# RWKV time mix inside a two-block network: the order of keys, decay, a, receptance, gate and values, scan inputs made during the values' products, mixed inputs kept in PSUM, two units of keys fed together

## The reference

```python
xx = jnp.pad(h, ((0, 0), (1, 0), (0, 0)))[:, :-1] - h
xm = h[None] + xx[None] * mix[:, None, None, :]
xr, xw, xk, xv, xa, xg = xm[0], xm[1], xm[2], xm[3], xm[4], xm[5]
r = xr @ w_r
k = xk @ w_k
v = xv @ w_v
w_log = -jax.nn.softplus(-(w0 + jnp.tanh(xw @ w1) @ w2)) - 0.5
a = jax.nn.sigmoid(a0 + (xa @ a1) @ a2)
g = jax.nn.sigmoid(xg @ g1) @ g2
kk = (k * k_k).reshape(B, T, H, N)
kk = kk / jnp.maximum(jnp.sqrt(jnp.sum(kk * kk, axis=-1, keepdims=True)), 1e-12)
k = k * (1.0 + (a - 1.0) * k_a)
decay = jnp.exp(-jnp.exp(w_log))
y = wkv7_scan(r, decay, k, v, -kk, kk * a)
bonus = (jnp.sum(rh * kh * r_k, axis=-1, keepdims=True) * vh).reshape(B, T, D)
```

## Time and profile before

| | us |
|---|---|
| median of 3 runs (lowest to highest) | 1727.52 (1726.04 to 1730.08) |
| the profiled execution, its own time | 1721.24 |
| its span, first to last instruction | 1719.50 |
| PE busy in the span | 1576.6 |
| DVE busy | 696.7 |
| ACT busy | 738.5 |
| POOL busy | 1089.1 |

### The profile page before, as it was taken

How to read it: one execution, slowest core, us unless ns; L and a number is a source line. 1 busy time by engine, 2 the same in 40 slices (tenths; PEclk the granted TensorE clock), 3 DMA queues, 4 the chain that set the end, 5 groups by cost and what they waited for, 6 DMA issues and landing times.

```text
span 1719.5 us, 40062 instructions
## 1 busy us (share of the span) xinstructions
PE 1576.6 (92%) x15940; PEld 1493.1 (87%) x15940; DVE 696.7 (41%) x1587; ACT 738.5 (43%) x1216; POOL 1089.1 (63%) x552
## 2 busy tenths in 40 slices
PE   6999969649998999999999988999988999879998
PEld 6999969628887999999999986699978987669998
DVE  4332065675445433213332287643341436443300
ACT  5444444423313444444444433654434534445532
POOL 5777848435403777787777752078867863338896
PEclk9999989769997999999999998999999999889999
DMA  6444623200011444454445642044546642215452
GB/s 237 172 178 145 206 101 138 79 0 2 3 52 50 157 178 171 151 199 172 171 148 168 200 149 74 2 157 173 188 115 190 225 146 98 75 53 193 175 210 80
DMA packets 38778, 231.28 MB, mean 135 GB/s; under 512 B 4511, under 2 KB 7680, under 8 KB 17552
## 3 DMA queue, kind: packets, MB, share of 16 engines
q1 hardware_dynamic: 34560, 225.49, 37.4%
q10 hardware_dynamic: 4112, 4.31, 1.3%
HBM read 227.09 MB, written 2.62 MB: 134 GB/s over the span
## 4 chain that ended last, share of the span: by engine, by line
PE 80%; DVE 8%; issue 7%; POOL 4%; ACT 1%; DMA 0%; SPq 0%; DVEq 0%; POOLq 0%; ACTq 0%
PE PS L744 66%; POOL wlo L693 4%; PE PS L743 2%; PE PS L927 1%; PE PS L942 1%; DVE score L2049 1%; PE PS L1296 1%; PE PS L934 1%; DVE prnb L2327 1%; PE PS L1087 1%; ACT whi L2405 0%; PE PS L1078 0%; PE PS L966 0%; PE PS L972 0%; PE PS L1272 0%
## 5 line engine op out<-in xcount | busy, mean ns | idle before, releaser
L693 POOL TENSOR_TENSOR wlo<-raw,whi 128x1024 fp32r<-128x1024 f32 (+1 forms) x472 | 1028.1, 2201 | 539.0 <-ACT whi L2405 486.2
L744 PE MATMUL PS<-xh,whi 128*128 128x272 f32 (+1 forms) x2336 | 681.9, 292 | 52.4 <-POOL wlo L693 23.0
L744 PE MATMUL PS<-xl,whi 128*128 128x272 f32 (+1 forms) x2336 | 674.4, 289 | 0.0
L744 PE MATMUL PS<-xh,wlo 128*128 128x272 f32 (+1 forms) x2336 | 673.6, 288 | 0.0
L2405 ACT ACTIVATE whi<-raw 128x1024 fp32r<-128x1024 f32 (+1 forms) x472 | 449.0, 982 | 281.7 <-PE PS L744 237.5
L744 PEld LDWEIGHTS PS<-xh,whi 128*128 128x128 f32 x2336 | 446.8, 191 | 61.8 <-issue 33.3
L744 PEld LDWEIGHTS PS<-xl,whi 128*128 128x128 f32 x2336 | 448.1, 192 | 0.3
L744 PEld LDWEIGHTS PS<-xh,wlo 128*128 128x128 f32 x2336 | 448.2, 192 | 0.0
L744 PE MATMUL PS<-hid_h,whi 128*128 128x272 f32 (+1 forms) x960 | 276.4, 288 | 16.8 <-POOL wlo L693 16.7
L744 PE MATMUL PS<-hid_h,wlo 128*128 128x272 f32 (+1 forms) x960 | 275.6, 287 | 0.0
L744 PE MATMUL PS<-hid_l,whi 128*128 128x272 f32 (+1 forms) x960 | 274.7, 286 | 0.0
(11 more groups left out here) (379 smaller groups left out, 1602.0 us busy)
## 6 DMA issues: line engine op xcount, KB each, us to landing
raw<-w_f_in_in SPq DMA_DIRECT2D x88, 1024.0 KB, 4.8
raw<-w_f_dn_in SPq DMA_DIRECT2D x64, 704.0 KB, 4.1
raw<-w_b_ff_in SPq DMA_DIRECT2D x32, 1024.0 KB, 4.8
raw<-w_rk_r_in SPq DMA_DIRECT2D x4, 1024.0 KB, 4.9
raw<-w_rk_k_in SPq DMA_DIRECT2D x4, 1024.0 KB, 4.7
raw<-w_rk_v_in SPq DMA_DIRECT2D x4, 1024.0 KB, 4.8
raw<-w_rk_o_in SPq DMA_DIRECT2D x4, 1024.0 KB, 4.9
raw<-w_at_q_in SPq DMA_DIRECT2D x4, 1024.0 KB, 4.9
```

The costliest lines, as they stand in the source:

```text
L693: nc.gpsimd.tensor_tensor(wlo[U % SPL][:, part], raw[U % RAW][:, part], whi[U % SPL][:, part].bitcast(F32), ALU.subtract).then_inc(s_lo, 1)
L744: mm(out, a, b, start=start and n == 0, stop=stop and n == 2, **kw)
```

## The change

The order of stages becomes keys, first factor of decay and a, receptance, second factor, gate, values. Line numbers in the rows below are each kernel's own.

```diff
-    ("rk_r", 4, 4, 2048), ("rk_k", 4, 4, 2048), ("rk_v", 4, 4, 2048),
-    ("lora_wa", 1, 1, 1024), ("lora_g", 1, 1, 1280), ("wa2", 1, 8, 1024),
+    ("rk_k", 4, 4, 2048), ("lora_wa", 1, 1, 1024), ("rk_r", 4, 4, 2048), ("wa2", 1, 8, 1024),
+    ("lora_g", 1, 1, 1280), ("rk_v", 4, 4, 2048),
...
+        def mixed_chunk(c):
+            return PS[:, 4 + c % 4, 0:T]
```

```diff
+                def first_two():
+                    U, G = U0[name], G0[name]
+                    pe.wait_ge(s_lo, 2 * (U + 2))
+                    pe.wait_ge(s_free, G)
+                    for k in range(KC):
+                        pe.wait_ge(s_x, X0[x] + k + 1)
+                        for u in range(2):
+                            for mi in range(2):
...
+                            if k == KC - 1:
+                                last.then_inc(s_unit, 2)
...
-            project("rk_r", T, 0, "m0")
-            project("rk_k", T, 1, "m1")
-            project("rk_v", T, 0, "m2")
+            project("rk_k", T, 1, "m0", wide=True)
...
+            project("rk_r", T, 3, "m3")
...
+            def spread_kk():
+                pe.wait_ge(s_kki, 1)
+                for c in range(KC):
+                    if c >= 4:
+                        pe.wait_ge(s_kkd, c - 3)
...
+            project("rk_v", T, 0, "m5", between=spread_kk)
```

VectorE: mixes are made in halves of four chunks, into PSUM, with four xh/xl buffers (indices 0 to 3; two more lie in tiles that are filled later), between the drains:

```diff
+            MIXES = ((2, 1), (1, 2), (4, 0), (0, 3), (5, 1), (3, 0))
...
-            mix(1, 2)
-            for u in range(4):
-                drain2("rk_r", u, R_[:, 2 * u:2 * u + 2, 0:T])
-            mix(2, 3)
+            mix(1, 0)
+            for u in range(2):
                 drain2("rk_k", u, K_[:, 2 * u:2 * u + 2, 0:T])
+            mix(1, 1)
+            mix(2, 0)
+            drain2("rk_k", 2, K_[:, 4:6, 0:T])
+            mix(2, 1)
+            drain2("rk_k", 3, K_[:, 6:8, 0:T])
+            mix(3, 0)
...
+            mix(3, 1)
...
+            mix(4, 0)
+            drain2("rk_r", 0, R_[:, 0:2, 0:T])
+            mix(4, 1)
+            drain2("rk_r", 1, R_[:, 2:4, 0:T])
+            mix(5, 0)
+            drain2("rk_r", 2, R_[:, 4:6, 0:T])
+            mix(5, 1)
```

The scan of the decays is made in eight pieces of 288; `wst` shrinks to one row of 288 and is cleared by VectorE. VectorE makes K_ x W_ and R_ x Wc itself, multiplies a_g by W_ before B_ is made (in place of B_ x W_ after), and drains the values between these steps. GpSimd's two whole-tile products and its clearing of `wst` are gone:

```diff
-                tt(K_[:, :, :], K_[:, :, :], W_[:, :, :], ALU.mult).then_inc(s_rks, 1)
-                tt(AR[:, :, :, 1, :], R_[:, :, :].rearrange("p c (b t) -> p c b t", t=BLK),
-                   Wc[:, :, :].rearrange("p c (b t) -> p c b t", t=BLK), ALU.mult).then_inc(s_rks, 1)
-                pool.wait_ge(s_rks, 2)
-                pool.wait_ge(s_bon, KC)
+                pool.wait_ge(s_we, 1)
+                pool.wait_ge(s_rks, 3)
+                pool.wait_ge(s_unit, 2 * U0["g2"])
...
+                if not half:
+                    dve.wait_ge(s_bonc, KC)
+                    v.tensor_tensor(bonus[:, :, :], bonus[:, :, :], V_[:, :, 0:T], ALU.mult).then_inc(s_bon, 1)
```

More of the change, by code:

```diff
@@ L754, in norm_sum, with project @@
                 mm(PS[:, 6, 0:n], ones[:, :], ss[:, 0:n], start=True, stop=True).then_inc(s_nmm, 1)
-            def project(name, n, b, x, norm=None, straight=0):
+            def project(name, n, b, x, norm=None, straight=0, wide=False, between=None):
+                def first_two():
[6 more added lines that the diff above has]
+                            for mi in range(2):
+                                c = mi * 1024 + k * 128
+                                last = products(PS[:, bank(G + u) + mi, 0:n], weights(U + u, ALLR, slice(c, c + 128)),
+                                                (xh[b][:, k, 0:n], xl[b][:, k, 0:n]), k == 0, k == KC - 1)
+                            if k == KC - 1:
+                                last.then_inc(s_unit, 2)
                 def body(us, i):
                     for u in us:
+                        if wide and u < 2:
+                            if u == 0:
+                                first_two()
+                            continue
+                        if between and u == 1:
+                            between()
                         U, G = U0[name] + u, G0[name] + u
@@ L1821, in _, with mix @@
-            for c0 in (0, 4):
-                shift(c0)
-                for c in range(c0, c0 + 4):
-                    mix_chunk(c, 0)
-                for c in range(c0, c0 + 4):
-                    dve.wait_ge(s_xh, X0["m0"] + c + 1)
-                    low(xl[0][:, c, :], xmf[:, c, :], xh[0][:, c, :], s_x)
-            for x in (R_, K_, V_, A_, B_):
+            MIXES = ((2, 1), (1, 2), (4, 0), (0, 3), (5, 1), (3, 0))
+            def mix(s, half):
+                which, b = MIXES[s]
+                if s == 4:
+                    dve.wait_ge(s_unit, 2 * U0["lora_wa"])
+                if s == 5:
+                    dve.wait_ge(s_unit, 2 * U0["rk_r"])
+                for c in range(4 * half, 4 * half + 4):
+                    n = X0[f"m{s}"] + c
+                    if n >= X0["m0"] + 4:
+                        dve.wait_ge(s_x, n - 3)
+                    v.scalar_tensor_tensor(mixed_chunk(c), xx[:, c, :], col(VEC["rk_mix"] + 8 * which + c), hn[:, c, :],
+                                           ALU.mult, ALU.add).then_inc(s_xm, 1)
+                for c in range(4 * half, 4 * half + 4):
+                    dve.wait_ge(s_xh, X0[f"m{s}"] + c + 1)
+                    low(xl[b][:, c, :], mixed_chunk(c), xh[b][:, c, :], s_x)
@@ L1829, in _ @@
+            for half in range(2):
+                shift(4 * half)
+                mix(0, half)
+            for x in (K_, A_, W_):
                 step.do(v.memset(x[:, :, T:TP], 0.0))
             step.sync()
-            mix(1, 2)
-            for u in range(4):
-                drain2("rk_r", u, R_[:, 2 * u:2 * u + 2, 0:T])
-            mix(2, 3)
-            for u in range(4):
-                drain2("rk_k", u, K_[:, 2 * u:2 * u + 2, 0:T])
-            mix(3, 1)
-            for u in range(4):
-                drain2("rk_v", u, V_[:, 2 * u:2 * u + 2, 0:T])
@@ L1898, in _ @@
             step.do(v.tensor_copy(a_to[:, :, :, 0:1], a_in[:, :, :, 0:1]))
[L1899 to L1905 removed]
+            v.tensor_tensor(a_to[:, :, :, 1:CH], a_in[:, :, :, 1:CH], decay[:, :, :, 0:CH - 1], ALU.mult).then_inc(s_rks, 1)
+            drain2("rk_v", 2, V_[:, 4:6, 0:T])
+            v.tensor_tensor(AR[:, :, :, 1, :], R_[:, :, :].rearrange("p c (b t) -> p c b t", t=BLK),
+                            Wc[:, :, :].rearrange("p c (b t) -> p c b t", t=BLK), ALU.mult).then_inc(s_rks, 1)
+            dve.wait_ge(s_ghh, 1)
+            low(gh_l[:, :, :], gh[:, :, :], gh_h[:, :, :], s_ghl)
+            drain2("rk_v", 3, V_[:, 6:8, 0:T])
+            step.sync()
             dve.wait_ge(s_rkc, 16)
```

228 lines of the change are left out of this document (118 added, 110 removed).

## The result

| | before | after |
|---|---|---|
| median of 5 runs, us | 1727.52 (1726.04 to 1732.00) | 1719.19 (1716.49 to 1722.44) |
| ratio, 95% interval | | 0.9947 (0.9926 to 0.9967) |
| profiled execution: own time, span | 1721.24, 1719.50 | 1720.92, 1719.1 |
| norm's sum to first transpose of the scan | 167.7 | 162.1 |

A forecast was written before the change was run, and what follows sets the result against it. The stage was taken as two halves: products first, then VectorE preparing the scan alone. First transpose 5.5 us earlier plus 1.0 at scan entry gave 6.5 less: 1714.7 profiled, predicted median 1721.0 us, range 1707 to 1733.

The forecast's parts named there:

- Front: Start through keys: splits hold VectorE's shift, first product moves from 227.17 to 230.8, TensorE waits 4.4 us, keys end at 261.1.
- Mixes: Mixes through receptance: splits hold mixes despite PSUM destination, low parts go free; TensorE waits 3.3 and 6.1 us.
- -3 to +3 us: Span allowed for 48 mixes written to PSUM, not shown by the trace, each taken as 0.42 us.
- my sum: First scan transpose 385.8 to 380.3, plus 1.0 at scan entry: 6.5 us less.
- Decay to values: Decay scan to second unit of values: A's multiply queued until 352.2, TensorE stops from 336 to 352.5, second unit at 356.0.
- Tail: Last VectorE work before the scan: B, A x decay and R x decay held once each; first transpose 380.3, 5.5 us earlier.
- Entry of the scan: Scan start: TensorE enters at full clock, not after 13.31 us of rest; gain taken as 1.0 us.
- Fewer holds: Rival behind 319: VectorE gets through between splits, 10.9 us of holds go, total 1710.1 us; chance 0.20.
- The clock stays low: Rival, third unit of keys to second of receptance: five units run at the low clock, total 1732.8 us; chance 0.17.
- Last inputs not hidden: Rival in the tail: B, A x decay and R x decay held twice each, 7.2 us more, total 1728.2; chance 0.18.
- The step from the sum to the median: Whole kernel: 1714.7 us for the profiled execution, plus 6.3 to the runs' median, gives 1721.0.

The follow-up runs named there:

- the units one after the other: Changed kernel with the first two units of keys fed one after the other, the second unit's cast behind the first mix; 1716.01 us, 0.9933 of before.
- the order alone: Changed kernel with mixed inputs back in SBUF and the first two units of keys one after the other, leaving the new stage order; 1718.37 us, 0.9936 of before.

## Why the prediction was right, and where it was not

- *Front.* Held shift, first product at 230.8: measured 230.64, the `hn` at 5.06 us. Third unit's drain at 248.9 after a wait of 4.4: 248.18 (the waiting product) and 3.94. Run with the units one after the other: the hold was the cause.
- *Mixes.* Holes of 3.3 and 6.1 us in receptance, ended by low parts: 2.04 and 4.48 (2.79 and 5.73 in the second profile). Mixes held beside splits with a PSUM destination: shown by 6.60 for four, and by 9.96 and 10.09 for the two destinations side by side. The 0.42 for a mix into PSUM was right (four take 1.74 where no split runs). But "-3 to +3 us" priced the mix alone as what PSUM may do, and left out the low part, which the walk of the mixes rightly took as not held any more. With two units fed together that is worth about 5 us of the stage. It stayed hidden in my sum, since I walked the queues with free low parts, so the total did not suffer; as a judgement on that part it was wrong.
- *Decay to values.* Scan in pieces with two holds 10.5: 9.60. A's multiply at 352.2: 351.02. Hole of 16 us before the fifth spread, second unit at 356.0: 16.45 and 355.33. The unit then took 8.3 us instead of 6.1: after that rest the granted clock was 0.50 up to 359; VectorE waited for it.
- *Tail.* Three holds, as counted, two on the operations named: A x decay (4.70) and R x decay (4.11). The third was on the copy of 72 columns (2.46 for 0.2) and not on B. First transpose 380.3: measured 380.29.
- *Entry of the scan.* This is the term that failed. I took a gain of 1.0 for a TensorE that enters at full clock. From the first transpose to the first level of the scan it did take less, 18.83, 18.80 and 18.89 us before, 17.15 and 17.16 after. But the levels of the scan's first half behind it took 18.10, 16.25 and 18.50 before and 20.81 and 21.10 after, since the granted clock fell in them for longer. At the end of that half the gain is gone: 36.9, 35.1 and 37.4 us from the first transpose before, 38.0 and 38.3 after. The bonus multiply ran inside the scan (2.38 us at 395.11), hidden.
- *Rivals.* "Fewer holds" is refuted by the rows: 9.60 for the decay scans, 7.57 for the bonus products. "The clock stays low" too: receptance ran at the higher level again from its second unit (granted clock 1.00 from 286 to 300). "Last inputs not hidden": three holds, not six.
- *The step from the sum to the median.* Here I was right by luck in part. At the output units the changed kernel led by 5.1 us, less than the 6.5 of the sum, and the medians differ by more. I took the 6.3 us between the profiled execution of before and its median as a constant. For the profiled execution I had 1714.7, and it was 1720.92; for the median 1721.0, and it was 1719.19. The first profile of before happened to have the short low parts and the short wait in attention; its second and third took 1724.49 and 1724.29. Even these are below their median of some 1728, and the rest, 3 to 4 us, was found in no profile. Nor do the profiles explain why the medians are 8.3 to 9 us apart, when the stage gives 6.4 (167.5 - 161.1) and the entry nothing. Both stay open.

## What to carry to other kernels

When two engines wait for each other in turn, look at what stands in the queue ahead of the one instruction that the other engine needs: moving eight small multiplies and a drain ahead gave as much as the new order of six stages. Before several edits go in together, undo each alone and in pairs, since here one of three cost 9 us without the second, and the second mostly repaired it. And take a stage's length from the trace and its time from many runs: one profile's distance from the median is not a constant.

## What was not expected of the hardware

VectorE operations with two SBUF inputs and GpSimd's splits mostly take turns instruction by instruction. Four low parts against four splits took 8.94 us (1.48 alone), eight multiplications against four splits 11.78 (3.39 alone), a whole-tile product of 2.5 us at most 4.71. So many small operations lose a turn each, and one large one loses one. Operations with one SBUF input that write SBUF wait as well: the copy of 72 columns before the change, and in the changed kernel the eight multiplications ahead of the new keys (5.37 us, where they took 2.23). A drain or a low part from PSUM does not: 1.49 for four beside the same splits that made 8.94. The Trainium skill (SBUF — State Buffer, section "SBUF: two separate sides") calls the shared port an exclusive lock; the rows agree, and show in addition that it mostly changes hands after each instruction when both engines have the next one ready.

Who gets the next turn is not fixed. Eight low parts starting 1.8 us ahead of a split took 2.91 us in two profiles and 7.23 to 7.25 in nine, with the same order and the same distance: the sixth low part and the split start together, within 0.01 us. In the two short ones three low parts went through in a row and the split waited instead. GpSimd's timeline of before, first profile:

```profile
547.67 3.37 POOL L693 TENSOR_TENSOR wlo<-raw,whi 128x1024 fp32r<-128x1024 f32 x1 [15.43 <-ACT whi L2405]
```

It takes 3.37 us where a split takes 2.4 alone. Behind the long form TensorE needed 166.5 to 169.2 us from the output units' first product to the feed-forward unit, behind the short one 163.7 and 164.5.

TensorE's granted clock fell within the scan's levels of 32 by 32 products in most profiles. In the changed kernel it fell behind a rest of 2.14 us (the next 118 products took 2.34 us), while in the run with the order alone the same 118 took 1.53 behind a rest of 2.41, so the rest alone doesn't decide it. In all eight profiles whose TensorE entered the scan at full clock but one, the first half's levels took 20.3 to 21.1 us; in the three of before, which entered with a mean granted clock of 0.58 or 0.59 over the first 6 us, they took 16.3 to 18.5. How long the lower level lasted varied too: windows of the first half in the changed kernel, then in the run with the units one after the other.

```profile
390.00:418.00 28.00, 25.04 (x1251) 23.74 (x1253) 14.70 (x36) 8.19 (x21) 16.71 (x25) 0.76 0.01 2
```

```profile
386.00:410.00 24.00, 21.05 (x1265) 19.80 (x1264) 14.52 (x36) 8.19 (x21) 15.98 (x25) 1.00 0.01 2
```

The same work took 20.8 us in the one (397.44 to 418.25) and 16.2 in the other (392.98 to 409.18). From the first transpose to the output units the thirteen profiles span 157.1 to 166.2 us. Behind the attention's index products, where all have the same code, they span another 4.7 us (714.5 to 719.2), which was not looked into. These stretches, and the turns above, are where the profiles differ, and so likely where the 4 to 15 us between executions of one kernel come from; what decides the clock there was not tried.
